# Moving the fourth unit of the gated convolution branch ahead of the normalised tiles, and four smaller moves of instructions, in a two-layer encoder trunk

## The reference, cut to what matters

```python
h = rmsnorm(x, norm_mix[i])
proj = h @ w_in[i]
q, k, v, cglu, sc_b, sc_c, sc_h, gates = jnp.split(proj, offs, axis=-1)
y_a = window_attention(q, k, v, attn_sinks[i], bias) @ w_attn_out[i]
ca, cb = jnp.split(cglu, 2, axis=-1)
c = ca * jax.nn.sigmoid(cb)
c = causal_dwconv(c, conv_dw[i]) + conv_dw_bias[i]
...
x = x + mix @ w_mix_out[i]
h2 = rmsnorm(x, norm_ffn[i])
x = x + (jax.nn.silu(h2 @ w_ffn_gate[i]) * (h2 @ w_ffn_up[i])) @ w_ffn_down[i]
gate = jax.nn.sigmoid(rmsnorm(x, norm_ple[i]) @ w_ple_gate[i])
x = x + (p[i] @ w_ple[i]) * gate
```

## Time and profile before

| | |
|---|---|
| median of 3 runs | 1130.98 us (1129.14 to 1131.5) |
| the profiled execution | 1129.25 us, span from first to last instruction 1127.4 us |
| mean granted TensorE clock | 0.995 of full speed |
| PE, DVE, ACT, POOL busy | 98%, 72%, 61%, 31% of the span |

### The profile page before, as it was taken

One profiled execution on the slowest core, in us unless ns is written; L12 is line 12 of the kernel. 1 busy time (PEld: TensorE's weight loads), 2 busy tenths in 40 slices (PEclk: granted clock), 3 DMA queues, 4 the chain that ended last, 5 costly groups with the idle time before them and its releaser, 6 DMA issues.

```text
span 1127.4 us, 18108 instructions
## 1 busy us (share of the span) xinstructions
PE 1106.0 (98%) x7202; PEld 1002.1 (89%) x7202; DVE 814.3 (72%) x1209; ACT 682.1 (61%) x1049; POOL 350.0 (31%) x319
## 2 busy tenths in 40 slices
PE   8899999999999999999989999999999999999997
PEld 8899899888898889889989989988888988998997
DVE  7987997898766554555799789878977665545554
ACT  6767875755746443445676788766475554334464
POOL 0787335874001000001129753458530100000011
PEclk9999999999999999999999999999999999999999
DMA  9564334555555545555545534355555455555541
GB/s 362 197 237 156 120 144 168 201 192 187 196 187 181 185 157 200 184 189 177 186 150 176 180 133 151 120 191 203 197 196 187 176 178 187 177 186 183 185 150 38
DMA packets 29347, 201.42 MB, mean 179 GB/s; under 512 B 3520, under 2 KB 3712, under 8 KB 5840
## 3 DMA queue, kind: packets, MB, share of 16 engines
q1 hardware_dynamic: 27648, 195.38, 49.4%
q0 software_dynamic: 1088, 4.74, 1.2%
q10 hardware_dynamic: 528, 0.15, 0.1%
HBM read 199.19 MB, written 3.69 MB: 180 GB/s over the span
## 4 chain that ended last, share of the span: by engine, by line
PE 90%; DVE 4%; ACT 3%; issue 1%; DMA 1%; SPq 0%; DVEq 0%
PE bank L393 15%; PE bank L395 15%; PE bank L394 15%; PE bank L355 14%; PE bank L356 14%; PE bank L357 14%; ACT w_hi L646 1%; DMA w_raw<-in_wstream 1%; DVE w_lo L1026 1%; PE bank L503 1%; PE bank L571 1%; PE bank L492 1%; PE bank L479 0%; PE bank L535 0%; ACT probs L772 0%
## 5 line engine op out<-in xcount | busy, mean ns | idle before, releaser
L1026 DVE TENSOR_TENSOR w_lo<-w_raw,w_hi 128x2048 fp32r<-128x2048 f32 x183 | 427.8, 2342 | 169.9 <-ACT w_hi L646 169.8
L646 ACT ACTIVATE w_hi<-w_raw 128x2048 fp32r<-128x2048 f32 (+1 forms) x185 | 350.7, 1899 | 116.3 <-DMA w_raw<-in_wstream 116.3
L1511 POOL TENSOR_TENSOR pacc<-pacc,cprod 128x256 f32<-128x256 f32 x224 | 253.1, 1130 | 124.8 <-ACT cprod L646 98.7
L355 PE MATMUL bank<-h_hi,w_hi 128*128 128x256 f32 x864 | 249.3, 289 | 6.1 <-issue 6.1
L356 PE MATMUL bank<-h_lo,w_hi 128*128 128x256 f32 x864 | 245.6, 284 | 0.0
L357 PE MATMUL bank<-h_hi,w_lo 128*128 128x256 f32 x864 | 245.5, 284 | 0.0
L393 PE MATMUL bank<-w_hi,h_hi 128*128 128x512 f32 x544 | 214.3, 394 | 0.0
L395 PE MATMUL bank<-w_hi,h_lo 128*128 128x512 f32 x544 | 212.1, 390 | 0.0
L394 PE MATMUL bank<-w_lo,h_hi 128*128 128x512 f32 x544 | 211.8, 389 | 0.0
L355 PE MATMUL bank<-act_hi,w_hi 128*128 128x256 f32 x608 | 173.8, 286 | 4.0 <-ACT qm L646 1.1
L355 PEld LDWEIGHTS bank<-h_hi,w_hi 128*128 128x128 f32 x864 | 166.8, 193 | 10.7 <-issue 10.7
(11 more groups left out here) (168 smaller groups left out, 1377.0 us busy)
## 6 DMA issues: line engine op xcount, KB each, us to landing
w_raw<-in_wstream SPq DMA_DIRECT2D x183, 1024.0 KB, 4.9
rel_bias_rows<-rel_bias_by_distance POOLq DMA_DIRECT2D x1, 2560.0 KB, 15.5
bias<-rel_bias_rows POOLq DMA_DIRECT2D x1, 1536.0 KB, 8.6
xs<-in_x SPq DMA_DIRECT2D x2, 512.0 KB, 5.6
w_raw<-in_wstream SPq DMA_DIRECT2D x2, 512.0 KB, 6.5
out_y<-xs SPq DMA_DIRECT2D x4, 256.0 KB, 2.4
zacc<-in_p POOLq DMA_DIRECT2D x2, 256.0 KB, 2.9
prms<-in_prm SPq DMA_DIRECT2D x1, 328.0 KB, 9.8
```

What stands on the lines that cost most here:

```text
L355: nc.tensor.matmul(o, wh, hi, start=first, stop=False, skip_group_check=True)
L646: return nc.scalar.activation(o, i, ACT.Identity, **kw)
L1026: nc.vector.tensor_tensor(w_lo[:, slot, :], w_raw[:, slot, :], f32(w_hi[:, slot, :]), ALU.subtract).then_inc(lo_ready, 1)
L1511: nc.gpsimd.tensor_tensor(o, a, cprod[:, n % PROD_RING, :], ALU.add).then_inc(pool_step, 1)
```

## The change

1. UNITS becomes 4: strips 0 to 7 use unscaled tiles, strip 8 is the first that needs normalised ones and waits for them. DVE does units 0 and 1 and the low part of chunk 3, then tiles 0 to 3, unit 2, tiles 4 to 7, unit 3. ACT takes the sigmoids of units 0 and 1 and the high part of chunk 3 first; the sigmoid of unit 2 stands between the two halves of `round_h`; the sigmoid of unit 3 stays in the loop, at t = 3.
2. In stage `sc`, at j = 1, ACT's `copy_probs(0)` stands ahead of `exponentials(1)`.
3. On ACT, chunks that were prepared ahead of the eight copies of `ple` are now prepared after the fourth.
4. On ACT, the chunk that was prepared in `ple_gate` at t = 5 is now prepared at the stage's end, together with the next.

```diff
--- before.py
+++ after.py
@@ -77,7 +77,7 @@
 CONV_W = SC_W + SC_WIDTH * DT
 G_NEXT = CONV_W + CONV_WIDTH * DT
 NPRM = G_NEXT + DT
-UNITS = 3
+UNITS = 4
 GA, GB = FA // 2, FB // 2
 GROUPS = GA + GB
 REL = 2 * SEQ // 2 + CHUNK
@@ -666,8 +666,8 @@
                 act.wait_ge(ms_ready, q + 1)
                 nc.scalar.activation(rstd[:, :], psum[4][:, 0:SEQ], ACT.Sqrt, bias=eps[:, :]).then_inc(std_ready, 1)
 
-            def round_h(q):
-                for t in range(DT):
+            def round_h(q, tiles):
+                for t in tiles:
                     act.wait_ge(hf_ready, q // 3 * DT + t + 1)
                     copy(h_hi[:, t, :], hf[:, t % 4, :]).then_inc(hhi_ready, 1)
 
@@ -737,12 +737,15 @@
 
                 root(L * 3)
                 raw_activate(0, 0, ACT.Sigmoid)
-                round_h(L * 3)
+                raw_activate(1, 2, ACT.Sigmoid)
                 round_chunk(L, AHEAD - 1)
+                round_h(L * 3, range(0, DT // 2))
+                raw_activate(2, 4, ACT.Sigmoid)
+                round_h(L * 3, range(DT // 2, DT))
                 for t in range(DT):
                     if t >= UNITS:
                         activate(t, 2 * t, ACT.Sigmoid, 2 * (t - 2) + 1)
-                    elif t > 0:
+                    elif t > 2:
                         raw_activate(t, 2 * t, ACT.Sigmoid)
                     if t > 0:
                         after_chunk(t - 1)
@@ -795,9 +798,11 @@
                     if j == 0:
                         exponentials(0)
                     after_chunk(C0["sc"] + j - 1)
+                    if j == 1:
+                        copy_probs(0)
                     if 0 < j < QT:
                         exponentials(j)
-                    if 0 <= j - 1 < QT:
+                    if 1 <= j - 1 < QT:
                         copy_probs(j - 1)
                     conv_products(before_sc + SC_PRODUCTS * j + SC_PRODUCTS // 2)
                     for s in (2 * j, 2 * j + 1):
@@ -965,12 +970,13 @@
                     strip_added("down_b")(t)
                     unscaled_high(t, G_PLE, h_hi)
                     square(L * 3 + 2, t)
-                for c in range(done, DT * FB // BPC - 1):
-                    after_chunk(C0["down_b"] + c)
                 for t in range(DT):
                     s = S0["ple"] + t
                     wait_strip(act, L, s)
                     copy(qm[:, t, :], psum[s % BANKS][:, 0:SEQ]).then_inc(bank_read[s % BANKS], 1)
+                    if t == 3:
+                        for c in range(done, DT * FB // BPC - 1):
+                            after_chunk(C0["down_b"] + c)
                     if t == PLE_AHEAD - 1:
                         root(L * 3 + 2)
                 after_chunk(C0["down_b"] + DT * FB // BPC - 1)
@@ -991,14 +997,13 @@
                         square(L * 3 + 3, t - 1)
                     if t == 3:
                         after_chunk(C0["ple_gate"])
-                    if t == 5:
-                        after_chunk(C0["ple_gate"] + 1)
 
                 for t in (DT - 2, DT - 1):
                     act.wait_ge(ple_added, L * DT + t + 1)
                     next_high(t)
                     square(L * 3 + 3, t)
-                after_chunk(C0["ple_gate"] + 2)
+                for c in (1, 2):
+                    after_chunk(C0["ple_gate"] + c)
                 load_root_table()
             act.wait_ge(ms_ready, 3 * DEPTH + 1)
             nc.scalar.activation(rstd_tok[:, :], psum[0][:, 0:TB], ACT.Sqrt, bias=eps[:, :]).then_inc(std_ready, 1)
@@ -1103,16 +1108,18 @@
                     nc.vector.tensor_tensor(o, psum[s % BANKS][:, 0:SEQ], gated[:, u % 2, :],
                                             ALU.mult).then_inc(bank_read[s % BANKS], 1)
 
+                def raw_unit(u):
+                    raw_gate(u, 2 * u)
+                    raw_product(cv[:, u, CPAD:], u, 2 * u + 1, u)
+
                 inverse(L * 3)
-                raw_gate(0, 0)
+                raw_unit(0)
+                raw_unit(1)
+                low_chunk(L, AHEAD - 1)
                 normalise_tiles(L * 3, L, G_MIX, range(0, DT // 2))
-                raw_product(cv[:, 0, CPAD:], 0, 1, 0)
+                raw_unit(2)
                 normalise_tiles(L * 3, L, G_MIX, range(DT // 2, DT))
-                raw_gate(1, 2)
-                low_chunk(L, AHEAD - 1)
-                raw_product(cv[:, 1, CPAD:], 1, 3, 1)
-                raw_gate(2, 4)
-                raw_product(cv[:, 2, CPAD:], 2, 5, 2)
+                raw_unit(3)
 
                 def after_chunk(c):
                     if c + AHEAD < CHUNKS or L < DEPTH - 1:
```

## The result

The changed kernel takes **1146.88 us** (1146.38 to 1148.26, 4 runs) beside 1130.17 us (1129.14 to 1131.5, 4 runs) of the kernel before: a ratio of 1.0147, with a 95% interval of 1.0135 to 1.0159. It is 16.7 us slower; 14.5 were forecast (1145.5 less 1130.98), and the time lies in the range of 1141.5 to 1149. The profiled execution has 1146.4 us, and its span 1144.6.

A forecast was written before the change was run, and what follows sets the result against it. PE, busy 98% of the span, was taken as the bound. 1129.25 + 7.6 (L0) + 7.6 (L1) + 0 (copies) - 0.6 (ple) = 1143.9, or 1145.5 us against the runs; forecast range 1143 to 1147.5, overall 1141.5 to 1149.

The forecast's parts named there:

- Units and chunk 3: At strip 6 in L0: chunk 3's low part done by 28.4, before PE wants it, removing the 3.85 us wait.
- The sigmoid behind the products: On ACT, unit 3's sigmoid waits behind chunks 4 and 5 and eight products; PE idles 11.4 us before strip 8 in L0.
- The sum: Added-up ACT, DVE and PE durations: sigmoid at 42.7, strip 8 at 46.3 in L0; whole profiled execution 1143.9 us.
- The low stretch: Half-clock stretch on PE after the new wait at strip 8, given the same 1.57 us as the one at strip 6.
- +7.6: Loss forecast in each of L0 and L1, by the later start of strip 9, in us.
- The copies: Stage sc: the wait for probs_t goes but returns as 2.0 us at the transposes; gain taken as 0 per layer.
- The copies' gain stays: Rival, stage sc: DVE's row is shortened too, up to 3.3 us return in both layers, 1142 to 1145; chance 0.08.
- The clock falls once more: Rival: half-clock after the sc wait, or longer at strip 8, up to 1.6 us per layer, 1146.5 to 1149; chance 0.11.
- Parts 3 and 4: In ple: waits for qm go; L1 gains 0.6 us, L0's gain goes into the next wait, shift within 0.5 us.
- The sigmoid isn't late: Rival: unit 3's sigmoid taken at once, strip 8 at 40.3, only +1.6 us per layer, 1133 us; chance 0.03.
- The rival of the other side: Rival: chunk 4's low part ahead of unit 3, strip 8 not waiting, all gains kept, 1120 us; chance 0.05.

The follow-up runs named there:

- e4: Changed kernel with ACT's first eight products moved behind unit 3's sigmoid, which still follows chunks 4 and 5; 1138.69 us, ratio 1.0066.
- e3: Changed kernel with unit 3's sigmoid on ACT moved ahead of chunks 4 and 5 and the eight products; 1135.72 us, ratio 1.0046.
- e5: Kernel before with only copy_probs(0) moved ahead of exponentials(1); 1130.56 us, ratio 1.0004.
- e6: Kernel before with copy_probs(0) ahead of exponentials(1), and low_attn(0) ahead of softmax(2) on DVE; 1129.89 us, ratio 0.9996.
- e7: Kernel before with copies ahead of exponentials at j = 1 and 2, and low_attn(0) ahead of softmax(2); 1130.85 us, ratio 0.9998.
- e1: Changed kernel with only UNITS 4 and its order kept, the copies and the two moved chunks put back; 1145.47 us, ratio 1.0129.
- e2: Kernel before with only the two moved chunks on ACT, UNITS still 3; 1129.24 us, ratio 0.9988.
- v1: Changed kernel with chunk 4 prepared early, its low part ahead of tiles 4 to 7 and unit 3's product; 1133.83 us, ratio 1.0031.
- v3: v1 with strips 8 and 9 taken as a pair, chunk 5 prepared early and DVE's taps moved later; 1125.93 us, ratio 0.9960.
- v2: v1 with low_attn(0) ahead of softmax(2) on DVE; 1132.45 us, ratio 1.0024.

## Why the prediction was right

**Units and chunk 3.** The wait at strip 6 is gone, as worked out; strip 6 follows strip 5 without a gap.

**The sigmoid behind the products.** The sum had it at 42.7 and the trace has 42.99 (the reciprocal alone is 0.26 later, 20.21 for 19.95), and the second four products, at 41.40, have no wait for POOL; DVE idles 6.43 us (about 6 were forecast); strip 8 at 46.69 (46.3). e4 takes the products away and e3 the chunks and products, and strip 8 follows: 46.69, 43.26, 41.92. The time follows too, if less exactly: 1146.88, 1138.69, 1135.72. The Trainium skill (TensorE: Matmul & The Clock Gate, section "Architectural detail: the array is 16× 32×32, not 1× 128×128") has ScalarE and VectorE work strictly in order; the trace agrees, with the sigmoid at 42.99 though its gate was made by 37.0.

**The low stretch was mis-sized.** The prediction gave "the same 1.57 us" to the stretch behind the wait of 11 us. In L0 it is 5.6 us at 0.50 and costs 2.5 us, and strip 8 starts 0.4 us later than summed. So +8.9 stands for +7.6 in L0. In L1 strip 8 starts 26.5 us behind the reciprocal (26.35 in the sum), its low stretch costs 1.8, and at strip 10 PE has lost 8.1 us by the reciprocal (16.5 less 8.4), not 7.6. That L1 adds just 7.6 to L0's +8.9 is luck: the moved chunks bring the reciprocal 0.5 us forward, which the sum had at nothing.

**Luck in the number.** The sum for the profiled execution was 1143.9 and it took 1146.4: 2.5 us too low, 1.3 in L0 and 1.5 in L1's `sc`. The forecast for the median added the 1.7 us by which before's median lay above its profiled execution; the changed kernel's lies only 0.5 above. That brought the forecast 1.2 us nearer to the median without a reason in the kernel.

**The copies.** The value of 0 was right, and the reason as given: e5 shows the wait going to L492, e6 and e7 show it going on from there to L503 and to three transposes. The wait was to be 2.0 us and is 1.9; the rows themselves give 1.65 + 0.16 = 1.8. "The copies' gain stays" is refuted, -1.7 and +1.8 us at the two places.

**The clock falls once more** was a rival with 1.6 us per layer. In the profiled run it came in one layer: 1.5 us in L1's `sc`, none in L0's. It explains why e1, without that stretch, takes 1.4 us less than the change. So this rival and the forecast both hold in part, and the time lies between them.

**Parts 3 and 4.** -0.8 us in L1's `ple` (-0.6 forecast). The gain of L0 goes into the next wait, but for the 0.5 us by which the reciprocal comes forward, at the edge of what I had allowed for the shift; that e2's stands 0.64 us later is its low stretch in `sc`.

**The sigmoid isn't late** is the rival that e3 makes real. It gave 40.3 for strip 8 and 1133 us; e3 has 41.92 and 1135.7, since the sigmoid waits for DVE's gate and chunk 4's high part stands behind it.

**The rival of the other side.** v1 is that rival made real, with chunk 4 ahead of unit 3, and it gives 1133.8 and not 1120. The step that fails is that all of the won wait would stay won: PE at strip 8 is then paced by DVE's tiles, and at 56 us waits for a bank. It took v3, with its pair of strips, to end below before, by 4.7 us with what parts 3 and 4 give.

## What to carry to other kernels

Where each engine works off a list in order, an instruction between two engines (here a sigmoid of 0.4 us) costs what stands ahead of it, not what it takes: list what is queued before it and price that. Before an order is changed to remove a wait, look at how busy the engine is that releases the next one: in stage `sc` DVE had next to nothing free, and three orders moved one wait of about 1.8 us from line to line for nothing. A matmul group that must start on late tiles ran better here as a pair of strips that share each tile than one by one (7.1 us for 8.6, v3 and v1).

## What the runs showed of the hardware

**The same idle gap may or may not bring the clock down.** The wait at L492 is 1.89 to 1.92 us in nine places of five kernels (the change, e3, e4, e5, two layers each, and v1's L1). Behind three of them the granted clock fell towards the 1.2 GHz level (0.57 in the change's L1, 0.65 and 0.75 in e4, whose stretches are read over 4 us), behind six it was 1.00. It isn't the length of the wait alone. Behind 1.66 us in e2's L0 the clock was 0.50, behind 1.65 to 1.67 us at the same line in before and e1 it was 1.00. Behind the 2.51 us at 56 in L0 it was 1.00 in v1 (50 to 60) and 0.71 in v2 (58 to 62). What decides it the runs don't settle. A fall in `sc` moved PE by 1.5 us each time, and e4's own runs lie 4 us apart, with mean clocks of 0.991 and 0.985.

**How much of a low stretch falls on work varies.** In the change the clock was already 0.50 in 38.7 to 46.6, while PE idled, and 5.6 us at 0.50 followed. In e1, behind the same wait, it was 0.50 in 46.6 to 51.3 and 1.00 from 51.4 on, and behind 3.85 us of idling it was 3.6 us at 0.53. The start times give 1.5 to 2.5 us as the price of one.

**DVE beside POOL.** In v1 DVE's tile operations at 35.72 and 36.59 took 0.95 us each where the next ones took 0.41 to 0.48, and its chunk 2.77 us where 2.29 is usual; POOL's add at 33.80 took 2.59 us where one takes 0.73 alone. The rows show whose turn it is: the one that starts second is the one that takes longer. The chunk at 33.03 starts 0.12 us behind POOL's add at 32.91, the add at 33.80 starts inside the chunk and ends 0.6 us behind it, and further on POOL's add starts inside a chunk that takes its usual time:

```profile
46.78 2.29 DVE L1033 TENSOR_TENSOR w_lo<-w_raw,w_hi 128x2048 fp32r<-128x2048 f32 x1
46.92 2.74 POOL L1522 TENSOR_TENSOR pacc<-pacc,cprod 128x256 f32<-128x256 f32 x1
```

The Trainium skill (GPSIMD Engine Reference, section "1. Specifications") says that GpSimd shares its SBUF interfaces with VectorE, with contention for DVE instructions with two SBUF inputs; the trace agrees, for these operations with two SBUF inputs.
